# Input projection of a two-group hybrid layer: first slab loaded in the block before, two slab banks, three modulation slabs, latent features modulated later

## What is computed

```python
m = silu(cond) @ w_mod + b_mod             # six vectors of 1024: shift, scale, gate, for two sub-layers
h = rmsnorm(x, norm_w) * (1 + scale) + shift   # cond: c for latent, c_ctx for context tokens
q, k, v, xr, yr = split(h @ w_in)          # w_in: 1024 x 2560
att = attention(q, k, v)                   # per group
rg_out = bidir_rglru(xr, yr, state, ...)   # conv, gates, two scans, times gelu(yr)
x = x + gate * (concat(att, rg_out) @ w_out)
...                                        # product-key experts, final norm
```

## Time and profile before

| | |
|---|---|
| median of 3 runs | 3749.11 us |
| the profiled execution: its own time | 3739.43 us |
| its span, first to last instruction | 3737.3 us |
| PE busy / VectorE / ScalarE / GpSimd | 84% / 71% / 28% / 53% of the span |
| mean granted clock of PE | 0.927 |
| mean DMA rate | 303 GB/s |
| context projection block | 54 to 214 us |
| dense and gathered experts, all of it | about 2000 to 3700 us |

### The profile page before, as it was taken

The page is one execution under the profiler, slowest core; times in us unless marked ns, Lnnn a source line. Parts: engine busy times, 40 slices in busy tenths (PEclk is TensorE's granted clock), DMA queues, the critical chain, the costliest instruction groups (busy, mean ns, idle before and its releaser), DMA issues. The chain is left out here.

```text
span 3737.3 us, 47455 instructions
## 1 busy us (share of the span) xinstructions
PE 3150.9 (84%) x15281; PEld 2082.0 (56%) x15281; DVE 2641.1 (71%) x5953; ACT 1045.5 (28%) x1817; POOL 1983.8 (53%) x1776
## 2 busy tenths in 40 slices
PE   5687699789859989377477899998999999999995
PEld 4446244556424333266355667676666666766663
DVE  2226788698475687999677778787777787886446
ACT  4441044366111000276311222222222222222112
POOL 0001565454245887222367677776777677776443
PEclk9888899899979999688788999999999999999997
DMA  6523577766577997258899999999999999999996
GB/s 244 201 85 120 170 265 248 215 214 215 221 251 284 314 339 246 102 172 245 315 379 374 353 408 408 404 405 382 409 399 408 381 405 404 408 405 378 366 345 240
DMA packets 411751, 1133.01 MB, mean 303 GB/s; under 512 B 34088, under 2 KB 129576, under 8 KB 411488
## 3 DMA queue, kind: packets, MB, share of 16 engines
q0 software_dynamic: 221184, 805.40, 57.7%
q1 hardware_dynamic: 174544, 317.82, 23.5%
q10 hardware_dynamic: 15888, 8.13, 0.7%
HBM read 1077.51 MB, written 53.71 MB: 303 GB/s over the span
## 5 line engine op out<-in xcount | busy, mean ns | idle before, releaser
L2272 POOL DMA_INDIRECT exp_value_row<-in_v_rows,exp_v_id x568 | 715.2, 1259 | 278.2 <-issue 176.1
L2319 DVE CUSTOM_DVE_ANT_0 edge_row<-edge_row,edge_x 128x1024 f32<-128x1024 f32 x480 | 583.6, 1218 | 289.0 <-DMA edge_row<-in_u_rows,edge_u_id 255.0
L2264 POOL DMA_INDIRECT edge_row<-in_u_rows,edge_u_id x480 | 508.2, 1059 | 329.2 <-DVE edge_dot L2319 178.3
L376 POOL DMA_INDIRECT ahead_row<-in_u_rows,keep_expert_id x256 | 336.3, 1314 | 347.8 <-DVE keep_dot L386 284.6
L2153 PE MATMUL exp_a_ps<-exp_xT_hi,exp_u_hi 128*128 128x512 f32 x1024 | 409.7, 400 | 19.1 <-DVE exp_u_lo L2288 10.0
L2168 PE MATMUL exp_o_ps<-exp_v_hi,exp_w_hi 128*128 128x512 f32 x1024 | 339.1, 413 | 80.5 <-DVE keep_acc L2383 80.3
L2153 PE MATMUL exp_a_ps<-exp_xT_lo,exp_u_hi 128*128 128x512 f32 x1024 | 401.5, 392 | 0.0
L2153 PE MATMUL exp_a_ps<-exp_xT_hi,exp_u_lo 128*128 128x512 f32 x1024 | 401.1, 392 | 0.0
L2383 DVE TENSOR_TENSOR keep_acc<-exp_o_ps,keep_acc 128x1024 f32<-128x1024 f32 x256 | 311.5, 1219 | 115.9 <-PE exp_o_ps L2168 114.6
L386 DVE CUSTOM_DVE_ANT_0 ahead_row<-ahead_row,ahead_x 128x1024 f32<-128x1024 f32 x256 | 304.0, 1220 | 76.6 <-DMA ahead_row<-in_u_rows,keep_expert_id 72.9
L2139 PE MATMUL exp_v_ps<-exp_value_row,exp_hot 128*32 128x512 f32 x2272 | 278.6, 602 | 60.5 <-DMA exp_value_row<-in_v_rows,exp_v_id 60.1
(11 more groups left out here) (380 smaller groups left out, 5134.3 us busy)
## 6 DMA issues: line engine op xcount, KB each, us to landing
edge_u_raw<-in_uT SPq DMA_DIRECT2D x130, 512.0 KB, 6.7
exp_v_raw<-in_v_rows SPq DMA_DIRECT2D x128, 512.0 KB, 6.7
exp_g_raw<-scratch_g SPq DMA_DIRECT2D x128, 256.0 KB, 8.3
scratch_g<-place_grid SPq DMA_DIRECT2D x3, 8192.0 KB, 36.2
proj_ctx_mod_slab<-in_w_mod SPq DMA_DIRECT2D x8, 2048.0 KB, 14.4
cheads_room<-in_w_in SPq DMA_DIRECT2D x10, 1024.0 KB, 5.1
heads_early_room<-in_w_in SPq DMA_DIRECT2D x10, 1024.0 KB, 9.7
exp_value_row<-in_v_rows,exp_v_id POOLq DMA_INDIRECT x568, 7.7
```

Source lines behind the costliest of these rows:

```text
L376: nc.gpsimd.indirect_dma_start(out=ahead.row[:, n % KEY_RING, :], out_offset=None, in_=io["u_rows"], in_offset=bass.IndirectOffsetOnAxis(a ...
L2264: nc.gpsimd.indirect_dma_start(out=key_row[:, j % RING, :], out_offset=None, in_=io["u_rows"], in_offset=bass.IndirectOffsetOnAxis(ap=u_id ...
L2272: nc.gpsimd.indirect_dma_start(out=value_row[:, 4 * (j % 2) + t, :], out_offset=None, in_=io["v_rows"].rearrange("a b n -> (a b) n"), in_o ...
L2319: nc.vector.tensor_tensor_reduce(out=key_row[:, j % RING, :], in0=key_row[:, j % RING, :], in1=x, scale=1.0, scalar=0.0, op0=ALU.mult, op1 ...
```

## The change

- Slab 0 of `w_in` is loaded in the modulation block, behind that block's own transfers, into `keep["acc"]`: half 1 at once, half 0 after all tiles are squared (the squares' scratch is its place).
- The context projection has two slab banks, `keep["acc"]` for slabs 0, 2 and 4 and the old room for slabs 1 and 3. Slab 1 is loaded at the block's start; slab `a + 2` goes out where slab `a + 1` did. The latent projection keeps one bank.
- `mod_slab` has three buffers. Three of its slabs are loaded at the block's start, the first ahead of slab 1, and later ones one by one: `load_mod(3 + 2a)` behind half 0 and `load_mod(4 + 2a)` behind half 1.
- In the modulation block only the context columns of `hT` are modulated. The latent ones follow in the context output projection, all eight feature tiles on ScalarE, behind the gate copies.

```diff
-def modulation_and_input_norm(nc, io, keep, hT):
+def modulation_and_input_norm(nc, io, keep, hT, early):
...
             for n in range(SLABS):
...
+            load_half(io, sp, early, 0, 1)
+            sp.wait_ge(squared, TILES)
+            load_half(io, sp, early, 0, 0)
         @block.gpsimd
         def _(pool):
...
-                for cnd, (at, width) in enumerate(((0, LATENT), (LATENT, CONTEXT))):
-                    if k % 2 == 0:
-                        last = nc.scalar.activation(hT[:, k, at:at + width], hT[:, k, at:at + width], ACT.Identity,
-                                                    scale=keep["factor"][:, 0, k, cnd:cnd + 1],
-                                                    bias=keep["mod_cols"][:, 0, k, cnd:cnd + 1])
-            last.then_inc(placed, 1)
+                if k % 2 == 0:
+                    modulate_columns(nc, keep, hT, CTX, k)
         @block.tensor
         def _(pe):
...
-                for cnd, (at, width) in enumerate(((0, LATENT), (LATENT, CONTEXT))):
-                    last = nc.vector.tensor_scalar(hT[:, k, at:at + width], hT[:, k, at:at + width],
-                                                   keep["factor"][:, 0, k, cnd:cnd + 1],
-                                                   keep["mod_cols"][:, 0, k, cnd:cnd + 1], ALU.mult, ALU.add)
-            last.then_inc(placed, 1)
+                nc.vector.tensor_scalar(hT[:, k, CTX.at:CTX.at + CTX.tokens], hT[:, k, CTX.at:CTX.at + CTX.tokens],
+                                        keep["factor"][:, 0, k, CTX.cond:CTX.cond + 1],
+                                        keep["mod_cols"][:, 0, k, CTX.cond:CTX.cond + 1], ALU.mult, ALU.add)
+def modulate_columns(nc, keep, hT, g, k):
+    at = slice(g.at, g.at + g.tokens)
+    nc.scalar.activation(hT[:, k, at], hT[:, k, at], ACT.Identity, scale=keep["factor"][:, 0, k, g.cond:g.cond + 1],
+                         bias=keep["mod_cols"][:, 0, k, g.cond:g.cond + 1])
 def modulation_rows(nc, keep, row_ps, slab):
...
-LATE_SLABS = 8
+LATE_SLABS, MOD_RING = 8, 3
 class Early:
-    def __init__(self, scope, signals, k_ctx):
-        self.room = scope.sb("room", [P, 2 * KD * SLAB // 2])
-        self.slab = [self.room[:, n * KD * SLAB // 2:(n + 1) * KD * SLAB // 2].rearrange("p (k n) -> p k n", k=KD)
-                     for n in range(2)]
+    def __init__(self, signals, name, k_ctx=None, first_bank=None):
+        self.banks = [self.halves(first_bank)] if first_bank is not None else []
+        self.count = len(self.banks) + 1
...
-        self.slab_in = [signals.sem(f"{scope.stage}_slab_in{n}") for n in range(2)]
-        self.k_in = signals.sem(f"{scope.stage}_k_in")
+        self.slab_in = [[signals.sem(f"{name}_slab_in{b}{n}") for n in range(2)] for b in range(self.count)]
+        self.k_in = signals.sem(f"{name}_k_in")
+    def hold(self, scope):
+        self.room = scope.sb("room", [P, KD * SLAB])
+        self.banks.append(self.halves(self.room[:, :]))
+    def halves(self, room):
+        half = KD * SLAB // 2
+        return [room[:, n * half:(n + 1) * half].rearrange("p (k n) -> p k n", k=KD) for n in range(2)]
+    def slab(self, a, n):
+        return self.banks[a % self.count][n]
+    def loaded(self, a, n):
+        return self.slab_in[a % self.count][n], 16 * (a // self.count) + 16
 def load_half(io, sp, early, a, n):
...
-    sp.dma_start(early.slab[n], io["w_in"].rearrange("(j p) n -> p j n", p=P)[:, :, a * SLAB + n * HALF:a * SLAB + (n + 1) * HALF])\
-      .then_inc(early.slab_in[n], 16)
+    sp.dma_start(early.slab(a, n), io["w_in"].rearrange("(j p) n -> p j n", p=P)[:, :, a * SLAB + n * HALF:a * SLAB + (n + 1) * HALF])\
+      .then_inc(early.slab_in[a % early.count][n], 16)
 def projection_and_rg_lru(nc, io, keep, g, hT, fused, v, early, ahead=None, units=(), spare=None):
...
-        slab, slab_in = early.slab, early.slab_in
...
-            mod_slab = s.sb("mod_slab", [P, 2, KD, SLAB])
+            mod_slab = s.sb("mod_slab", [P, MOD_RING, KD, SLAB])
...
-            mod_in = [s.sem(f"mod_in{n}") for n in range(2)]
+            mod_in = [s.sem(f"mod_in{n}") for n in range(MOD_RING)]
...
             def load_mod(n):
-                if n >= 2:
-                    sp.wait_ge(rows_made, n - 1)
+                if n >= MOD_RING:
+                    sp.wait_ge(rows_made, n - MOD_RING + 1)
...
-                sp.dma_start(mod_slab[:, n % 2, :, :], w_mod[:, :, at:at + SLAB]).then_inc(mod_in[n % 2], 16)
-            if context:
-                load_half(io, sp, early, 0, 0)
+                sp.dma_start(mod_slab[:, n % MOD_RING, :, :], w_mod[:, :, at:at + SLAB]).then_inc(mod_in[n % MOD_RING], 16)
             sp.dma_start(cols[:, 0:RG_ROWS, :], io["rg_cols"]).then_inc(cols_in, 16)
             if context:
-                load_half(io, sp, early, 0, 1)
+                load_mod(0)
+                for a in range(1, early.count):
+                    load_half(io, sp, early, a, 0)
+                    load_half(io, sp, early, a, 1)
             else:
                 sp.dma_start(early.k_ctx, io["k_ctxT"]).then_inc(early.k_in, 16)
             load_weights(0)
             load_weights(1)
             if context:
-                load_mod(0)
                 load_mod(1)
+                load_mod(2)
             for a in range(SLABS):
-                sp.wait_ge(made, 4 * a + 2)
-                load_half(io, sp, early, a + 1, 0)
-                if context and a >= 1:
-                    load_mod(2 * a)
-                    load_mod(2 * a + 1)
-                sp.wait_ge(made, 4 * a + 4)
-                load_half(io, sp, early, a + 1, 1)
+                ahead_slab = a + early.count
+                if ahead_slab <= SLABS:
+                    sp.wait_ge(made, 4 * a + 2)
+                    load_half(io, sp, early, ahead_slab, 0)
+                if context and MOD_RING + 2 * a < LATE_SLABS:
+                    load_mod(MOD_RING + 2 * a)
+                if ahead_slab <= SLABS:
+                    sp.wait_ge(made, 4 * a + 4)
+                    load_half(io, sp, early, ahead_slab, 1)
+                if context and MOD_RING + 2 * a + 1 < LATE_SLABS:
+                    load_mod(MOD_RING + 2 * a + 1)
                 if 1 <= a < RG_TILES - 1:
                     sp.wait_ge(product, PRODUCTS * a)
                     load_weights(a + 1)
...
-                        pe.wait_ge(slab_in[ct // 2], 16 * a + 16)
+                        pe.wait_ge(*early.loaded(a, ct // 2))
...
-                                                slab[ct // 2][:, k, ct % 2 * P:(ct % 2 + 1) * P],
+                                                early.slab(a, ct // 2)[:, k, ct % 2 * P:(ct % 2 + 1) * P],
...
             def late_rows(n):
-                pe.wait_ge(mod_in[n % 2], 16 * (n // 2) + 16)
+                pe.wait_ge(mod_in[n % MOD_RING], 16 * (n // MOD_RING) + 16)
...
-                modulation_rows(nc, keep, row_ps[n % 2], lambda k: mod_slab[:, n % 2, k, :]).then_inc(rows_made, 1)
+                modulation_rows(nc, keep, row_ps[n % 2], lambda k: mod_slab[:, n % MOD_RING, k, :]).then_inc(rows_made, 1)
             def late_columns(n):
...
-                        pe.wait_ge(slab_in[half], 16 * (SLABS + 1))
+                        pe.wait_ge(*early.loaded(SLABS, half))
...
                     else:
...
-                                                hT[:, k, g.at + t * P:g.at + (t + 1) * P], slab[half][:, k, :],
+                                                hT[:, k, g.at + t * P:g.at + (t + 1) * P], early.slab(SLABS, half)[:, k, :],
...
             if context:
...
+            if context:
+                for k in range(KD):
+                    modulate_columns(nc, keep, catT, LAT, k)
             act.wait_ge(eps_ready, 1)
...
-                modulation_and_input_norm(nc, io, keep, featT)
+                early = Early(s, "cheads", first_bank=keep["acc"].rearrange("p t n -> p (t n)"))
+                modulation_and_input_norm(nc, io, keep, featT, early)
...
-                    early = Early(h, s, None)
+                    early.hold(h)
...
-                    early = Early(e, s, keep["acc"][:, 3, :].rearrange("p (j n) -> p j n", j=4))
+                    early = Early(s, "heads_early", k_ctx=keep["acc"][:, 3, :].rearrange("p (j n) -> p j n", j=4))
+                    early.hold(e)
```

More of the change, by code:

```diff
@@ L163, in modulation_and_input_norm @@
         factor_ready = s.sem("factor_ready")
-        placed = s.sem("placed")
         own = s.sem("own_vector")
```

## The result

| | before | changed |
|---|---|---|
| median, us | 3747.9 (3741.89 to 3754.56, 4 runs) | 3701.57 (3700.84 to 3711.23, 4 runs) |
| ratio, 95% interval | | 0.989, 0.987 to 0.9909 |
| span of the profiled execution | 3737.3 | 3699.9 |

The medians differ by 46.3 us, where 44.9 were forecast. The two profiled spans differ by 37.4 only. The forecast gain stands in the stage that was changed; where the other 7 us of the profile went is told further down. That the medians agree with the forecast within 1.4 us is in part luck, for the runs of one kernel scatter by 10 to 13 us.

What follows compares the result with a forecast made beforehand. PE and bus waited for each other in the context projection, held by SP's issue order; 7.9 + 31.9 + 7.1 - 2.0 = 44.9 us off 3739.4 gives 3694.5, forecast 3704 on the median's level, range 3688 to 3719.

Steps and rivals of the forecast that it cites:

- 31.9 us of stalls: Context projection, slabs 1 to 3: PE's three waits for late modulation slabs, 10.60, 10.57 and 10.77 us, go.
- 7.1 us of lower clock: Context projection: half-speed clock after the three stalls, 4.0 + 1.45 + 1.65 us, comes back with them.
- It was SP's order, not room, that held it: Context projection: modulation slab 2, issued at 92.01, had its buffer free since about 73.3.
- rival b: Context projection: ScalarE and VectorE become the bound, three slabs slipping 4 us each; gain 33, 3716 us; chance 0.08.
- 7.9 less 2.0: Context projection's start: slab 1 at 75.2 instead of 83.12 gains 7.9 us; clock relapse after the new wait costs 2.0.
- a sign of being wrong: Context projection: the prediction called itself wrong if, among other signs, rows 0 wait.
- The new wait ahead of rows 1: Context projection's start: PE idles 3.4 us until modulation slab 1 lands at 72.4, paid in full.
- 4.75 MB at a flat 384 GB/s: Context projection's start: transfer rate that put modulation slab 0 in at 60.0 and slab 1 at 72.4.
- rival (a): Context projection's start: transfers not in issue order, modulation slab 0 in at 77.8, gain falls 18 to 27, 3722 us; chance 0.07.
- bounds of 1.45 to 4.0: Context projection, after the new wait: price of one clock relapse if it occurs, otherwise 0; 2.0 us taken.
- the stages behind 214 us: All after the context projection: keep their old length, else the prediction is wrong.
- Rival (d): Dense expert stretch: starts earlier and is granted less clock, slower; at 0.04 less, 3765 us; chance 0.03.

Runs made afterwards that it cites:

- order only: Kernel before with only SP's issue order changed, late modulation slabs going out one by one; median 3751.68 us beside 3789.0, ratio 0.9893.
- and weights first: Changed kernel with modulation slab 1 and the first RG-LRU weights issued ahead of projection slab 1's halves; median 3747.98 us, ratio 0.9886 to the kernel before.
- shared ring: Changed kernel with three modulation buffers shared by both blocks, late slabs 0 and 1 issued in the modulation block; median 3743.77 us, ratio 0.9864 to before.
- changed again: Changed kernel run once more without edit, on the second chip of the experiments; median 3754.13 us, ratio 0.9891 to the kernel before.
- activations twice: Changed kernel with the output projection's eight latent-column activations made once more into an unread tile; one run, 3752.88 us.
- latent in the block: Changed kernel with all columns, latent ones too, modulated in the modulation block again; median 3752.39 us, ratio 0.9897 to the kernel before.
- banks, old pairs: Changed kernel with a modulation ring of two and SP's old paired order for late modulation slabs; median 3787.35 us beside 3789.0, ratio 0.9993.
- slab 1 of modulation first: Changed kernel with modulation slab 1 issued ahead of both halves of projection slab 1; ratio 0.9881 to the kernel before.

## Why the prediction was right, step by step

**The stalls.** The 31.9 us of stalls were to go and did, and the 7.1 us of lower clock with them: the whole of slabs 1 to 3 took 64.3 us in the changed kernel (77.91 to 142.20), 21.4 a slab, and 21.5 was the figure. "It was SP's order, not room, that held it" is shown by the run with the order alone. ScalarE and VectorE did not become the bound (rival b); in that run and the changed one the neighbourhood of fourth and fifth slot runs without idle time.

**The start.** PE at 49.76 (49.8), rows 0 at 59.74 (60.0), slab 1 at 77.91 (75.2, and 77.2 with the relapse). The gain at slab 1's start was 5.2 us, where 7.9 less 2.0 had been summed; 4.3 of it are the earlier end of ScalarE's tail. Rows 0 waited 1.35 us, which the prediction had named as a sign of being wrong, though its own sum had 0.4 there (59.6 to 60.0). It is a small one: the slab came on time and PE was early, its first 32 matmuls taking 8.63 us for 9.80. The new wait ahead of rows 1 was 4.92 us and not 3.4. PE was there at 68.76 (69.0), so it is modulation slab 1 that came 1.3 us late. The step that was mis-sized is 4.75 MB at a flat 384 GB/s behind modulation slab 0, 12.4 us, for which 13.94 went (59.74 to 73.68):

```profile
60.00:65.00 5.00, 5.00 (x32) 3.28 (x25) 0.80 (x2) 0.60 (x1) 0.00 (x0) 1.00 1.09 350
65.00:70.00 5.00, 3.77 (x18) 2.98 (x16) 0.00 (x0) 0.77 (x2) 0.00 (x0) 1.00 1.05 384
70.00:75.00 5.00, 1.32 (x8) 0.40 (x12) 0.00 (x0) 0.00 (x0) 0.00 (x0) 0.83 1.05 387
```

In the first of these windows, in which by the order of issue slab 1's halves land, the bus moves 350 GB/s; that costs 0.4 us. And the 13.94 us hold 5.2 MB by these rows (350 and 384 GB/s for 5 us each, 387 for the last 3.7, and 0.1 MB ahead of 60), some 0.45 MB or 1.2 us more than the order puts ahead of modulation slab 1's end. The likely reading is that this much of what comes behind was already moving; the rows do not tell one transfer's bytes from another's. So the order of issue held in the mean with a blur of some 0.45 MB, and rival (a), which needed the whole batch, did not occur. The Trainium skill, "DMA: Bandwidth & Descriptors", section "Two DMAs through the same engine are not ordered", says that one queue's descriptors start in order and that nothing orders transfers across the 16 engines. By this rule, the trace agrees: order in the mean, and a blur, here some 0.45 MB, that the rule leaves open.

**The clock.** Taken at 2.0; it was 1.46 in the changed kernel's profile (rows 1 took 3.38, 73.68 to 77.91 is 4.23 and 2.77 at full speed). In the other profiles it cost more. From the start of rows 1 to the first value matmul it took 67.6 us in the three kernels in which PE waited for nothing on this way ("order only", "and weights first" and the shared ring), 69.0 in the changed kernel, 71.9, 71.6 and 71.5 in "changed again", "activations twice" and "latent in the block". In "banks, old pairs", up to the end of the fourth slot, it took 15.6 us where the shared ring took 11.15. So a wait of 4.3 to 4.9 us was followed by the slow clock in all five (rows 1 took 3.38 to 3.64 us for 1.92), at 1.4 to 4.5 us each. The prediction's bounds of 1.45 to 4.0 were a little too narrow, and the 2.0 in the sum fitted the profile of the result better than the others.

**The level.** Up to SP's first issue for the latent projection the profile gained 44.3 us, at the end 37.4. The 6.9 us in between are 3.8 up to the gathered rows' stores and 3.0 in the dense stretch. The prediction had said that it would be wrong if the stages behind 214 us changed their length; by these few us they did. In the ten profiles the stage from SP's first issue for the latent projection to those stores took 1689.5 to 1701.1 us, and the kernel before had the shortest: its profiled execution was also the fastest of its kernel. So the 3.8 us are within what executions differ by. The sum held up to the latent projection, 44.3 us for 44.9.

**Rival (d)** did not occur. The dense stretch (from the stores of the gathered rows to the final norm) took 1596.8 us before and 1599.8 changed in the runs of the result, 1643.5 to 1645.8 on the first chip of the experiments, whether it began at 2095 or at 2047: its length did not depend on its start. Windows 2100 to 3600 of three kernels, before, order only and changed again, show what differs:

```profile
2100.00:3600.00 1500.00, 1430.05 (x6999) 1015.61 (x6997) 1111.32 (x1536) 348.03 (x480) 1031.01 (x953) 0.99 1.01 396
```

```profile
2100.00:3600.00 1500.00, 1402.48 (x6807) 997.78 (x6806) 1077.45 (x1490) 336.98 (x466) 991.13 (x927) 0.98 0.99 384
```

```profile
2100.00:3600.00 1500.00, 1397.67 (x6795) 992.86 (x6794) 1072.84 (x1485) 334.94 (x462) 993.38 (x925) 0.98 0.99 383
```

The stretch is 3% longer in the runs of the experiments. The granted clock is 0.99 and 0.98, and PE's busy time per instruction is 204.3, 206.0 and 205.7 ns, 0.7 to 0.8% apart; what grew is PE's idle time, 70 us of 1500 before, 98 and 102 in the two others. So PE's own work explains a quarter or so of the 3%. The DMA engines are busy for nearly the whole of it in each (0.99 to 1.01) and move 396, 384 and 383 GB/s. That makes the bus the likely bound, but it is not shown: PE is busy for 93 to 95% too, and a lower mean rate follows from a longer stretch whatever makes it longer. No run here varied it, and since each chip was measured at one time only, chip and time can't be told apart either. The expectation of "changed again", less than 5 us of difference between kernels of one chip, failed with 1640.0 to 1650.6; since "changed again" and "activations twice" share every instruction behind 245 us and differ by 2.3 us, part of it at least is scatter between executions, and the rest is open.

## What to carry to other kernels

When a ring stalls, look first at the issuing engine's own order: a transfer may be queued behind a wait that has nothing to do with its buffer. Here that took seven lines to mend and was worth 39 of 45 us, while two banks, the early fetch and the moved latent columns without that order were worth nothing that a total could show. Sum what must land before each consumer, in the order of issue, and give the first place to what is asked for first: the early fetch brought at most a microsecond as long as the next transfer was late, 6 us once modulation slab 1 went first, and 7.5 with the weights ahead too. And verify parts of a few us at marks inside the timeline; what lies behind them, 1690 to 1701 us of other stages and a dense stretch of 1600, scatters by more than they are worth.

## What was not expected of the hardware

In the three sets of runs the same program, the kernel before, had medians up to 1.4% apart (3747.9, 3789.0 and 3798.6 us), and the two profiles of the changed kernel, 46.1 us apart, put the difference in the dense stretch (1599.8 and 1648.3 us), while the changed kernel reached the latent projection within 0.3 us of the same time.

The same queue moved less while the half slabs landed, whose pieces are 1 KB (256 columns of 4 bytes), than with modulation slabs, whose pieces are 2 KB. In the changed kernel the low window is 60 to 65 us, 350 GB/s beside 384 and 387. In "and weights first", where the halves stand one modulation slab and the weights further back, 65 to 70 is the low one:

```profile
60.00:65.00 5.00, 5.00 (x30) 3.63 (x23) 0.47 (x1) 0.78 (x2) 0.00 (x0) 1.00 1.05 382
65.00:70.00 5.00, 5.00 (x31) 2.91 (x30) 0.00 (x0) 0.59 (x2) 0.00 (x0) 1.00 1.09 349
```

The low window moved with the halves. It is also at 65 to 70 us in "slab 1 of modulation first" (352 GB/s) and at 55 to 60 in the shared ring (351), where the halves come behind two modulation slabs. That it is the size of the pieces and not something else in these transfers was not varied.
